# First norm of a fused two-block kernel: where the squares are made and summed, and who makes the second weight unit's low part

## What is computed

```python
def rmsnorm(x, g):
    x32 = x.astype(jnp.float32)
    y = x32 * lax.rsqrt(jnp.mean(x32 * x32, axis=-1, keepdims=True) + RMS_EPS)
    return (y * g).astype(x.dtype)

h = rmsnorm(x, norm1_g[l])
p = h @ w_in[l]
p_rwkv, q, k, v, gate_logits = jnp.split(p, IN_SPLITS, axis=-1)
```

## Time and profile before

| what | value |
|---|---|
| median of three runs | 1907.99 us (1901.94 to 1912.77) |
| span of the profiled execution, first to last instruction | 1907.8 us |
| TensorE matmul busy | 1794.9 us, 94% |
| VectorE busy | 996.6 us, 52% |
| ScalarE busy | 652.1 us, 34% |
| GpSimd busy | 350.4 us, 18% |
| mean granted TensorE clock | 0.978 |

### The profile page before, as it was taken

One profiled execution on the slowest core, in us unless ns is written; L12 is line 12 of the kernel. 1 busy time (PEld: TensorE's weight loads), 2 busy tenths in 40 slices (PEclk: granted clock), 3 DMA queues, 4 the chain that ended last, 5 costly groups with the idle time before them and its releaser, 6 DMA issues. The chain is left out here.

```text
span 1907.8 us, 44979 instructions
## 1 busy us (share of the span) xinstructions
PE 1794.9 (94%) x19187; PEld 1327.8 (70%) x19187; DVE 996.6 (52%) x1844; ACT 652.1 (34%) x1233; POOL 350.4 (18%) x508
## 2 busy tenths in 40 slices
PE   6999989999989979999989999989998999999998
PEld 5777667777766763343357776767777787888887
DVE  7666445555467641121177865756667674323334
ACT  5455443534323222221145632021212343213421
POOL 1000054524344421101000000013222011001100
PEclk9999999999999979989999999999998999999999
DMA  6222111101149579999971213510001423332331
GB/s 228 81 92 75 58 62 42 37 31 42 53 133 366 189 290 380 409 408 407 409 267 56 67 34 126 182 56 15 25 11 62 166 90 121 99 99 89 99 99 45
DMA packets 76430, 267.18 MB, mean 140 GB/s; under 512 B 11408, under 2 KB 13840, under 8 KB 74832
## 3 DMA queue, kind: packets, MB, share of 16 engines
q1 hardware_dynamic: 65040, 236.02, 34.2%
q10 hardware_dynamic: 5616, 15.99, 2.4%
q0 software_dynamic: 5584, 12.40, 1.8%
HBM read 250.27 MB, written 21.50 MB: 142 GB/s over the span
## 5 line engine op out<-in xcount | busy, mean ns | idle before, releaser
L218 DVE TENSOR_TENSOR weights_lo<-ring,weights_hi 128x1024 fp32r<-128x1024 f32 (+1 forms) x134 | 165.7, 1239 | 146.5 <-ACT weights_hi L214 146.5
L214 ACT CAST weights_hi<-ring 128x1024 fp32r<-128x1024 f32 (+1 forms) x134 | 137.0, 1025 | 240.3 <-PE ps L244 228.4
L243 PE MATMUL ps<-wide_b_round,weights_hi 128*128 128x512 f32 (+1 forms) x368 | 135.4, 368 | 0.0
L242 PE MATMUL ps<-mlp_hi,weights_hi 128*128 128x512 f32 (+1 forms) x327 | 121.3, 371 | 1.2 <-DVE weights_lo L218 1.1
L244 PE MATMUL ps<-mlp_hi,weights_lo 128*128 128x512 f32 (+1 forms) x327 | 120.5, 368 | 0.0
L243 PE MATMUL ps<-mlp_lo,weights_hi 128*128 128x512 f32 (+1 forms) x327 | 120.4, 368 | 0.0
L242 PE MATMUL ps<-wide_a_round,weights_hi 128*128 128x512 f32 x216 | 91.7, 424 | 0.6 <-DVE wide_b_round L735 0.6
L242 PE MATMUL ps<-h_tail,weights_hi 128*128 128x512 f32 x232 | 91.4, 394 | 0.7 <-DVE weights_lo L218 0.6
L244 PE MATMUL ps<-h_tail,weights_lo 128*128 128x512 f32 x232 | 91.1, 393 | 0.0
L243 PE MATMUL ps<-h_tail_rest_round,weights_hi 128*128 128x512 f32 x232 | 90.4, 390 | 0.0
L4589 POOL TENSOR_TENSOR h_scaled<-h_scaled 128x512 f32<-128x512 f32 x32 | 33.8, 1056 | 297.9 <-ACT h_scaled L4563 297.9
(11 more groups left out here) (694 smaller groups left out, 4195.1 us busy)
## 6 DMA issues: line engine op xcount, KB each, us to landing
ring<-stream_in SPq DMA_DIRECT2D x207, 512.0 KB, 3.4
moe_ring<-stream_in SPq DMA_DIRECT2D x112, 512.0 KB
wide_b<-stream_in SPq DMA_DIRECT2D x32, 512.0 KB
w_mod<-w_mod_in ACTq DMA_DIRECT2D x24, 512.0 KB, 6.6
xT<-w_mod_in SPq DMA_DIRECT2D x16, 512.0 KB, 4.3
gates_parked<-gates_late SPq DMA_DIRECT2D x14, 256.0 KB, 2.6
na_rel<-rel_in POOLq DMA_DIRECT2D x4, 640.0 KB, 4.2
xT<-xT_in SPq DMA_DIRECT2D x4, 512.0 KB, 5.8
```

What stands on the lines that cost most here:

```text
L214: act.copy(self.hi[:, i % self.n, at:], w[:, at:]).then_inc(self.cast.sem, self.cast.up())
L218: ins = eng.tensor_tensor(self.lo[:, i % self.n, at:], self.unit(i)[0][:, at:], self.hi[:, i % self.n, at:], ALU.subtract)
L242: pe.matmul(out, left[0], right[0], start=start, stop=False, **kw)
L243: pe.matmul(out, left[0], right[1], start=False, stop=False, **kw)
```

## The change

GpSimd, ahead of its DMA issues, squares block 6 into `raw[:, 0]`, and then, when the first unit's low part is made, makes the low part of weight unit 1. ScalarE squares blocks 0 to 5 as before, and block 7 into `raw[:, 1]`, with no wait for an add. VectorE adds blocks 1 to 5, and makes the low part of unit 0 only; before its loop over the later units it waits until two units are counted as used. TensorE adds up three partial sums of squares in PSUM: `sq[:, 0]`, block 7 and block 6, four matmuls each, where it had one sum of four.

```diff
+            last_squared, pool_squared = k.sig("last_squared"), k.sig("pool_squared")
...
+                def sum_part(x, first, last):
+                    for t in range(NT):
+                        mm = pe.matmul(k.ps[32 * t:32 * t + 32, 6, 0:P], k.c("ones")[:, 0:32], x[:, t * P:(t + 1) * P], start=first, stop=last)
+                    return mm
+
                 pe.wait_ge(got.sem, got.at(32))
-                norm.sum(pe)
+                pe.wait_ge(norm.added.sem, norm.added.at(DB - 3))
+                sum_part(norm.sq[:, 0, :], True, False)
+                pe.wait_ge(last_squared.sem, last_squared.at(1))
+                sum_part(raw[:, 1, :], False, False)
+                pe.wait_ge(pool_squared.sem, pool_squared.at(1))
+                sum_part(raw[:, 0, :], False, True).then_inc(norm.summed.sem, norm.summed.up())
                 keep_busy(k, pe, 3, 0)
                 norm.spread(pe)
                 keep_busy(k, pe, 9, 0)
...
-                for b in range(DB):
+                for b in range(DB - 2):
                     if b % 2 == 0:
                         act.wait_ge(x_in[b // 2].sem, x_in[b // 2].at(16))
                     norm.square(act, b, k.xT[:, b, :])
+                act.wait_ge(x_in[3].sem, x_in[3].at(16))
+                act.activation(raw[:, 1, :], k.xT[:, DB - 1, :], ACT.Square).then_inc(last_squared.sem, last_squared.up())
                 norm.root(act)
...
-                for b in range(1, DB):
+                for b in range(1, DB - 2):
                     norm.add(dve, b)
                 norm.invert(dve)
                 w.rest(dve, 0)
-                w.rest(dve, 1)
...
+                dve.wait_ge(k.used, 2)
                 for u in range(len(units)):
...
                 pool.wait_ge(x_in[3].sem, x_in[3].at(16))
+                x = k.xT[:, DB - 2, :]
+                pool.tensor_tensor(raw[:, 0, :], x, x, ALU.mult).then_inc(pool_squared.sem, pool_squared.up())
+                pool.wait_ge(k.used, 1)
+                w.rest(pool, 1)
                 pool.dma_start(mask[:, :], k.dram["na_mask"]).then_inc(rel_in.sem, rel_in.up(16))
```

## The result

| | kernel before | changed kernel |
|---|---|---|
| median of 20 runs each, on the same chip | 1906.81 us (1900.51 to 1913.22) | 1912.01 us (1904.13 to 1919.3) |
| ratio, with its 95% interval | 1 | 1.003 (1.0018 to 1.0042) |
| span of the profiled execution | 1907.8 us | 1902.3 us |
| mean granted TensorE clock in it | 0.978 | 0.981 |

The change makes the kernel 0.3% slower, 5.7 us by the ratio. That is less than the half per cent that counts as a change here, and it lies in the predicted range; but it is more than the 0.15 us that the sum gave. Note first that the profiled execution of the changed kernel is its fastest: 1904.13 us in time with a span of 1902.3, next to a median of 1912.01. So spans can't be compared for the size of the loss. The traces are read for their mechanisms, the size is read from the medians.

A forecast was written before the change was run, and what follows sets the result against it. TensorE, busy 94%, was taken as the bound, so only the moment from which it runs without a gap counts. Span 1907.8 + 0.15 = 1908.0; with the median 0.2 above the span, 1908.2; range 1902 to 1914.

The forecast's parts named there:

- the 0.15 us that the sum gave: Total of the forecast's terms: TensorE's first product starts 0.15 us later and the end moves by as much.
- a chance of 0.91: Chance given to a time that counts as the same, beside faster 0.03 and slower 0.06.
- Squares and adds: Start, ahead of the sum: add 5 and GpSimd's square in sequence end at 11.28, level with the columns; at most 0.55 us gained.
- Three sums: TensorE's sum in the norm: 0.40 us per further part (bounds 0.23, 0.65), from 11.40 to 12.85, so 0.22 us later.
- The spread: TensorE's eight spread records behind the sum: up to 0.5 us shorter if closer spacing starts sooner, which wouldn't help.
- The low part on GpSimd: GpSimd makes weight unit 1's low part from 15.55 to 17.92; `rest_x(0)` is held and ends at 18.48.
- Rival (b): GpSimd fetches code for its first elementwise operation, up to +14.6 us unless hidden ahead of the wait for x; chance 0.07.
- The first product: TensorE's first product matmul: starts at 18.63 against 18.48, +0.15 us.
- What else moves: Mask and bias loads queued behind GpSimd's new work, ring unit 7 and later waits: no effect on the time.
- TensorE hands it on unchanged.: Behind the first product, TensorE passes the start's +0.15 us through to the kernel's end.
- TensorE idle time past 20 us that wasn't there: A sign that would show the forecast wrong: new TensorE idle time later than 20 us.
- The span: Profiled execution before: 1907.8 us, with the median of three runs, 1907.99, taken as 0.2 above it.

The follow-up runs named there:

- its second run: The changed kernel, without further edit, compared once more with the kernel before: 1908.31 us, ratio 1.0009.
- the kernel with the sums alone: Against the kernel before, only the new squares and three partial sums; VectorE still makes both low parts: 1911.73 us, ratio 1.0032.
- 32 fewer: The changed kernel with its twelve small fillers around the spread replaced by three longer and one small: 1903.72 us, 0.9986; repeated on another chip 1906.57 us, 0.9993.
- The kernel with 64 more: The kernel before with 128 waits without work ahead of TensorE's first wait, making 64 records more: 1906.0 us, ratio 0.9996.

## Why the prediction was right, and where it was wrong

**The forecast.** 1908.2 with 1902 to 1914; measured 1912.01. Within half a per cent, as put with a chance of 0.91. The mechanism behind that 0.91, a price of 0.15 us, is not what moved the median. The range held a term that it doesn't name because it was as wide as the spread of the runs; as far as the mechanism goes, that is luck.

**Squares and adds.** Add 5 and the square one behind the other were to be done at 11.28; the adds ended at 11.30 (6.77 + 4.53) and the sum began at 11.45, where 11.40 was forecast. The terms weren't those of the forecast, so the near hit is partly luck: the square took 1.36 beside VectorE's adds, above the 1.04 to 1.19 that I took from other rows, but began at 9.39 and not at 9.57. It ended at 10.75, and add 5 ended 0.55 later, as `rest_x(0)` did behind the weight unit. That the columns are level with the adds is shown by the releasers of the sum: VectorE (11.45) in the change, the columns in its second run (11.30) and in the kernel with the sums alone (11.26).

**Three sums.** The further parts were priced at 0.20 per step and strip, and the second part followed the first 0.40 later (11.45, 11.85); in all 1.51 (11.45 to 12.96) against 1.45 forecast. The ends of the range, 0.23 and 0.65 per part, were both wrong, and the spacing in the very instructions that were tripled was the right row. The spread was shorter, 1.39 for 1.90, and that didn't help, as the forecast said.

**The low part on GpSimd.** 15.55 to 17.92 forecast, 15.56 to 17.93 measured. `rest_x(0)` was held as said: 1.22 in place of its own 0.69, ending 0.55 behind GpSimd, while the two scalings beside it kept their 1.41. The Trainium skill ("SBUF — State Buffer", Who interferes with whom) says that a VectorE instruction with two SBUF inputs contends with a GpSimd instruction that reads SBUF, and one with at most one SBUF input doesn't; both rows agree. Rival (b), code to be fetched for GpSimd's first operation, isn't seen: the square started at 9.39, upon the landing of x. Its two configuration instructions stand ahead of that wait, which is the cover of which the rival spoke; whether anything was loaded beneath it no row shows.

```profile
L808 POOLq MODIFY_POOL_CONFIG  x2: 11/11/11, 0.8 to 0.8; - x2
```

**The first product.** +0.15 forecast, +0.14 in the first pair of traces. The repeats forbid taking this for precision: before started it at 18.48 and 18.60, the changed kernel at 18.62, 18.48 and 18.53. The means are 18.54 and 18.54. The price of the stage is nothing within 0.1 us: the sum ends 0.33 later (12.96 for 12.63), and `scale_x(0)` no longer has a second low part in front of it, so it still starts 0.38 sooner (15.83 for 16.21).

**What else moves.** GpSimd's mask add was the first user of what was queued behind the new work; it started at 26.97 for 26.83, 0.14 later like the products, and waited for VectorE's last `rest_x` and not for a DMA. Nothing, as forecast.

**"TensorE hands it on unchanged."** This is the step that failed. I priced the 16 added matmuls by their time in the sum. I didn't ask what their records do to everything behind them, although "TensorE idle time past 20 us that wasn't there" stood among the signs of being wrong, and it is this sign that came: 2.46 us at 533 us. In place of a start that moves the end by +0.15 the runs show a start that doesn't move (18.54 in both means) and, with 32 records more, +0.22% in the mean of five comparisons; the kernel before with nothing but such records shows it too (1.0025). The stretch behind the longest gap is 4.6 us longer, but other stretches are shorter, so it isn't shown to be where the median's loss arises.

**The span.** I took the profiled execution of before for the median less 0.2 us. Where a run's time and span are both known, they are 1.8 to 1.9 apart in the seven profiled executions that hold a part of the change and 2.2 to 2.3 in the six that don't. So the profiled execution of before took some 1910.0. It was an ordinary run, 2 us above the median of the three and 3 above that of the 20. Why a part of the change takes 0.4 us from what lies outside the span isn't found.

**What stays open.** That the packet at each gap carries the block TensorE waits for is inferred, from the size, the counts and the constant distance; no row names it. Shown is that 32 records without work make gap and loss (1.0025), and that 32 fewer undo both. Open is the way from the records to the median: the gap at 533 us is one of many that move, its stretch doesn't make the five traces longer as a whole, and there is one trace for each kernel. Why the clock falls with the longer gap and not with the shorter ones isn't shown either. The kernel with 64 more, which loses 2.0 us here and nothing in its ratio, suggests that what is lost at one block's end can be won elsewhere. And the three comparisons of the change differ (1.0030, 1.0009, 1.0015), so its size is known as 0.1 to 0.3%.

## What to carry to other kernels

By these runs an instruction can have a second price beside its time: it moves every later instruction of its engine against the places where the engine waits for nothing that the profile shows. Where a program has dense groups of very small matmuls, count the records that an edit adds ahead of them, look for idle time with the releaser "issue" inside such groups in both traces, and measure the edit once with the count held as it was. For effects under half a per cent take the kernel against itself and two comparisons at least, and look at the same stretch in all traces. Take that stretch wide as well as narrow: here 48 us around the gap told the two sorts of kernels apart cleanly, and from the first product on the difference was gone.

## What the runs showed of the hardware

- Gaps of TensorE with no releaser stand at the same record numbers (16,577 and 16,833, and others a multiple of 256 away) whatever instruction is there, and at these two they end 2.3 to 2.9 us behind the start of a 16,384-byte instruction packet. Packets start 3.2 us apart at the closest. That the records come in blocks of 256, and that TensorE waits where it runs them down faster than packets follow, is inferred from this.
- Such a gap of 1.9 to 2.5 us came with 10.2 us at the granted clock 0.50 in all five kernels that had it at this place; with gaps of 0.4 to 0.95 us the stretch stayed at 1.00, save for two times 3.4 us at 0.50, from 538.6 and 569.3 on, in one (the change with 32 fewer). From the group to the later matmul that is a difference of 4.6 us; from the first product to there it is 0.3.
- Two waits on a semaphore in a row make one record in TensorE's queue: 34 waits added 17 records, 64 added 32, 128 added 64.
